# Rotary halves exchanged by transfers, and stacked high and low query parts for the grouped heads, in a two-block transformer kernel

## The chip, the cores and the metric

One core of a Trainium2 chip runs the whole program. The metric is the device time of one execution in microseconds (us). The kernel before takes 2801.74 us, the median of three runs (2801.63 to 2803.39).

## The reference

A sequence of 512 tokens of width 1024 goes through two mixing layers of a first block (`attn0`, `attn1`) and then through six stages of a second block (four gated feed-forward stages, a state-space mixer, a convolution mixer). All is float32. The change touches the attention of the two mixing layers only:

```
proj = rms_norm(x) @ w_in           # split into dq dk dv dgate gq gk gv ggate mq mgate
dq, dk  = rope(dq), rope(dk)        # 6 heads of 2x32, halves of 16 rotated
gq = axial_rope(rms_norm(gq))       # 6 query heads of 64, in groups of 3
gk = axial_rope(rms_norm(gk))       # 2 key heads of 64
def rope(x):  x1, x2 = halves(x); return concat(x1*cos - x2*sin, x2*cos + x1*sin)
oa = softmax(q1 k1') v - lam * softmax(q2 k2') v      # 6 differential heads
ob = softmax(gq gk') v                                # 6 grouped heads
om = softmax(mq mk') mv                               # 4 memory heads, 256 keys
x = x + rms_norm(concat(oa, ob, om) * silu(gates) @ w_out)
```

## The kernel before

**Split products.** Float32 operands of the large products are split into a leading part of reduced precision (type fp32r) and a low part, the difference. A product is the sum of three: high by high, high by low, low by high. `mm3` (lines 418 to 423) issues them for the projections, lines 1949 to 1951 for the scores.

**Projections.** The activations lie with their 1024 features in the partitions (`XH`, `XL`). `w_in` comes in 12 blocks of 256 columns, loaded to two alternating buffers `raw` by SyncE's queue (`load_block`, line 410: the load waits until VectorE has used the buffer). ScalarE writes the leading part `WH` (line 383), VectorE the low part `WL` (line 388), TensorE does 48 products of 512 columns into two banks, and VectorE evicts each bank with the norm factor to a tile of `PR` (lines 2257 and 2259). Blocks are counted two higher in the weight order from the fifth on, since two blocks of `w_mem_kv` come between; so `low_w(12)`, `low_w(13)` and `low_w(14)` on VectorE are the low parts of block 10, block 11 and the first block of `w_out`. Block 11 (the memory queries) is multiplied inside the unit loop, by `queries` in the first five units.

**Rotation.** Ten tiles turn: six of the differential heads (`ROPED[0]` to `[5]`) and, after their norm (`head_norm`, line 2292), the three tiles of grouped queries and one of grouped keys (`ROPED[6]` to `[9]`). TensorE's `swap(n)` (line 1878) multiplies a tile by a permutation that exchanges rows 16 apart and leaves it in bank 6 or 7. VectorE's `turn(n)` multiplies the tile by the cosine (line 2301), the exchanged tile by the signed sine (line 2302), and adds (line 2304). The turns stand between the evictions and the low parts of the weights in VectorE's written order: turns 0 and 1 after `low_w(8)`, 2 and 3 after `low_w(9)`, 4 and 5 after `low_w(10)`, 6 and 7 after `low_w(11)` and the four head norms, 8 and 9 after `low_w(12)`.

**Grouped keys.** Heads whose rows don't match their key head's rows read a copy `gk2` of the keys with the halves changed (lines 2333 and 2334), announced by `ready`. ScalarE's `lead_qk` (line 2112) writes the leading parts of all queries and keys, GpSimd's `low_qk` (line 1820) the low parts.

**Unit loop.** A unit is one head and one tile of 128 queries: 24 differential units (two score sets each), 24 grouped, 16 memory. For each, TensorE makes scores (lines 1949 to 1951), VectorE their maxima (line 2346), ScalarE the exponentials (line 2180), VectorE reciprocals (line 2361), GpSimd scales (lines 1828 and 1830, or 1837), TensorE transposes (line 1978) three units later, ScalarE or VectorE copies to `PT` (lines 2190, 2355), and TensorE multiplies by the values every second unit (line 1992). Every engine runs its part in the written order of units; semaphores tie them. Three norm products stand at unit 42 (line 1959).

Of the kernel before, what the change touches and what calls it, by code (L numbers as in the profile page):

```python
# [96 lines left out]
def program(nc, io, stages=FULL):  # L97
    ctx = ExitStack()
    with ctx:
# [185 lines left out]
        y_scr = nc.dram_tensor("y_scr", [KD, P, CL, NC], F32).ap()  # L285
        tab_scr = nc.dram_tensor("tab_scr", [P, TAB], F32).ap()
        mm_scr = nc.dram_tensor("mm_scr", [12, P, 72, 32], F32).ap()
        z_scr = nc.dram_tensor("z_scr", [3, 4, P // 4, 4, P], F32).ap()
        k_scr = nc.dram_tensor("k_scr", [2, LAGS, P], F32).ap()
        cs_scr = nc.dram_tensor("cs_scr", [KD, P, 2, GS, NC + 1], F32).ap()  # L290
# [45 lines left out]
        def col(name, k, n=0):  # L336
# [8 lines left out]
                        rstd_ok=1, ysq_dve=1, ystat_ok=2, yrms_ok=2, ycol_ok=2, ybc_ok=2, xn=2 * KD),  # L345
            "ffn": dict(silu=KF, hid=KF, hh=KF, hl=KF, ysq_in=9, ysq_use=7, ysq_dve=1),
            "attn": dict(mem_in=32, rope_in=16, mem_n=2, ml=KD, mem_t=KD, mh=KD, mrms=1, msq=2, vm_t=1, vmh=1, vml=1,
                         v_t=4, vh=4, vl=4, gsq=4, gms=4, gln=4, grms=4, gn=4, swapped=10, roped=10, ready=1, gate=8,
                         s=91, e=91, nb=64, p=24, pn=40, rsum=64, scaled=24, qh=14, ql=14, pt=64, pt_a=52, pt_d=12, pv=32, o=16, osq=3, orms=3, og=3,
                         mixh=KD, mixl=KD, ysq_in=8, ysq_use=7, wpart=2),  # L350
            "s5": dict(z=KD, wt=KD, h2=KD, l2=KD, ysq_in=8, ysq_use=7, wpart=2),
            "conv": dict(ysq_in=8, ysq_use=7, wpart=2),
# [1241 lines left out]
        def head(h):  # L1594

            if h < 6:
                parts = [(DQ + h // 2, DK + h // 2, 0, (h % 2) * 64 + 32 * i, 32) for i in range(2)]
                c = (h // 2) * P
                return parts, (lambda s: Vd[:, s, c:c + P]), 4, DG + h // 2
            if h < 12:  # L1600
                g = h - 6
                kv, row = g // 3, (g % 2) * 64
                return ([(GQ + g // 2, GK if kv * 64 == row else "gk2", 0, row, 64)],
                        (lambda s: Vg[:, s, kv, :]), 4, GG + g // 2)
            g = h - 12
            c = (g // 2) * P
            return ([(MQ + g // 2, "MK", (g // 2) * NMEM, (g % 2) * 64, 64)],
                    (lambda s: Vm[:, s, c:c + P]), 2, MG + g // 2)
# [52 lines left out]

        def ms_buf(n):
            return PR[:, (22, 23, 18, 19)[n], :]

        def norm_buf(n):
            return sq[:, n, :] if n < 2 else ssq[:, :]
# [120 lines left out]
        def attn_sp(sp, s):  # L1787
            b0, l = first_block[s], int(s[4])
            wm = io["w_mem_kv"][l].rearrange("(k p) n -> p k n", p=P)
            wi = io["w_in"][l].rearrange("(k p) n -> p k n", p=P)  # L1790

            def in_block(n):
                a = BLOCKS[n][0] * P
                load_block(sp, b0 + n + (2 if n >= 4 else 0), n % 2, raw3(n % 2, KD), wi[:, :, a:a + 2 * P])

            for n in range(4):
                in_block(n)
            if s == stages[0]:
                par_sp(sp, s)
            for q in range(2):  # L1800
                load_block(sp, b0 + 4 + q, q, raw3(q, KD), wm[:, :, q * 256:(q + 1) * 256])
            for n in range(4, 12):
                in_block(n)
            out_sp(sp, b0 + 14, io["w_out"][l])

        def attn_pool(pool, s):
            l = int(s[4])
            if before(s) is None:
                x_all(pool, s)
            pool.dma_start(MEMN[:, :, :], io["mem"][0].rearrange("(t p) d -> p t d", p=P)).then_inc(ss(s, "mem_in"), 16)  # L1810
            pool.dma_start(perm[:, :, :], io["perm_c"]).then_inc(ss(s, "mem_in"), 16)
            squares_pool(pool, s)
            pool.wait_ge(mm_done, first_step[s] + 12)
            pool.dma_start(rope[:, :, :], io["rope_c"]).then_inc(ss(s, "rope_in"), 16)

            def low_qk(n):

                x, high, low, _, _ = SPLIT[n]
                pool.wait_ge(ss(s, "qh"), at(s, "qh", n + 1))
                pool.tensor_tensor(low, x, high.bitcast(F32), ALU.subtract).then_inc(ss(s, "ql"), 1)  # L1820

            for n in range(12):
                low_qk(n)
            for u in range(DIFF_UNITS):
                m = SCORE0[u]
                pool.wait_ge(ss(s, "scaled"), at(s, "scaled", u + 1))
                e1, e2 = E[:, slot(m), :], E[:, slot(m + 1), :]
                pool.tensor_tensor(e2, e2, stats[:, 3, (m + 1) % 8:(m + 1) % 8 + 1].to_broadcast([P, T]), ALU.mult)
                pool.drain()  # L1829
                pool.tensor_tensor(e1, e1, e2, ALU.add).then_inc(ss(s, "p"), 1)  # L1830
                if u in QUERY_ACT:
                    low_qk(12 + QUERY_ACT[u])
            for u in range(DIFF_UNITS, len(UNITS)):
                m, nk = SCORE0[u], HEADS[UNITS[u][0]][2]
                pool.wait_ge(ss(s, "rsum"), at(s, "rsum", u + 1))
                e = E[:, slot(m), 0:nk * P]
                pool.tensor_tensor(e, e, stats[:, 3, m % 8:m % 8 + 1].to_broadcast([P, nk * P]), ALU.mult)\
                    .then_inc(ss(s, "pn"), 1)
            out_pool(pool, s)

        def attn_pe(pe, s):
# [26 lines left out]
                    mm = pe.transpose(bank[4][:, t * P:(t + 1) * P], PR[:, VALUES[n], t * P:(t + 1) * P], ident[:, :])  # L1868
                mm.then_inc(ss(s, "v_t"), 1)

            def swap(n):

                j = ROPED[n][0]
                if j >= GQ:
                    pe.wait_ge(ss(s, "gn"), at(s, "gn", j - GQ + 1))
                if n >= 2:
                    pe.wait_ge(ss(s, "roped"), at(s, "roped", n - 1))
                pe.matmul(bank[6 + n % 2][:, :], perm[:, 0, :], PR[:, j, :], start=True, stop=True)\
                  .then_inc(ss(s, "swapped"), 1)

            in_pair(pe, s, b0, j0)

            def mem_turns(n0, n1):
# [16 lines left out]
                                      ident[:, :])  # L1900
            mm.then_inc(ss(s, "vm_t"), 1)
            pe.wait_ge(ss(s, "mem_in"), at(s, "mem_in", 32))
            swap(0)
            swap(1)
            block(5)
            swap(2)
            swap(3)
            pe.wait_ge(ss(s, "vmh"), at(s, "vmh", 1))
            value_turn(0)
            head_squares(0)  # L1910
            block(6, lambda: head_squares(1))
            swap(4)
            swap(5)
            value_turn(1)
            head_squares(2)
            block(7, lambda: head_squares(3))
            value_turn(2)
            block(8, lambda: (swap(6), swap(7)))
            value_turn(3)
            block(9, lambda: (swap(8), swap(9)))  # L1920
            block(10)
            pe.wait_ge(l_done, b0 + 11 + 2 + 1)
            pe.wait_ge(ss(s, "roped"), at(s, "roped", len(ROPED)))
# [9 lines left out]
            def scores(u):  # L1933
                h, t = UNITS[u]
                if t == 0:
                    pe.wait_ge(ss(s, "ql"), at(s, "ql", 6 if h < 6 else 11 if h < 12 else 14))
                for i, (q, k, k0, row, n) in enumerate(HEADS[h][0]):
                    m = score(u, i)
                    keys = HEADS[h][2] * P
                    (qh, ql), (kh, kl) = [[x[row:row + n, c:c + w] for x in QK[name]]  # L1940
                                          for name, c, w in ((q, t * P, P), (k, k0, keys))]
                    acc = score_bank(u, i)[:, 0:keys]
                    if u >= MEM_U:
                        pe.wait_ge(ss(s, "e"), at(s, "e", m - 2))
                    elif m >= 4:
                        pe.wait_ge(ss(s, "e"), at(s, "e", m - 3))
                    else:
                        pe.wait_ge(acc_read, j0 + min(25 + m, 26))
                    pe.matmul(acc, qh, kh, start=True, stop=False)
                    pe.matmul(acc, qh, kl, start=False, stop=False)  # L1950
                    pe.matmul(acc, ql, kh, start=False, stop=True).then_inc(ss(s, "s"), 1)  # L1951
# [91 lines left out]
        def attn_act(act, s):  # L2043
# [59 lines left out]
            def lead_qk(n):  # L2103
# [5 lines left out]
                    act.wait_ge(ss(s, "ready"), at(s, "ready", 1))  # L2109
                if n >= 12:  # L2110
                    act.wait_ge(acc_read, j0 + 26 + n - 12 + 1)
                act.activation(high, x, ACT.Copy).then_inc(ss(s, "qh"), 1)

            def silu(n):
# [121 lines left out]
        def attn_dve(dve, s):  # L2236
# [25 lines left out]
            def low_w(n):  # L2262
                split_l(dve, b0 + n, n % 2, 16)
# [31 lines left out]
            def turn(n):  # L2295

                j, tab = ROPED[n]
                if n == 0:
                    dve.wait_ge(ss(s, "rope_in"), at(s, "rope_in", 16))
                dve.wait_ge(ss(s, "swapped"), at(s, "swapped", n + 1))  # L2300
                dve.tensor_tensor(PR[:, j, :], PR[:, j, :], rope[:, tab, :], ALU.mult)
                dve.tensor_tensor(work1[:, n % 2, :], bank[6 + n % 2][:, :], rope[:, tab + 1, :], ALU.mult)
                dve.drain()
                dve.tensor_tensor(PR[:, j, :], PR[:, j, :], work1[:, n % 2, :], ALU.add).then_inc(ss(s, "roped"), 1)

            if s == stages[0]:
                par_angle_dve(dve, s)
# [22 lines left out]
            evict(9)  # L2330
            low_w(13)
            dve.drain()
            dve.tensor_copy(gk2[64:128, :], PR[0:64, GK, :])
            dve.tensor_copy(gk2[0:64, :], PR[64:128, GK, :])
            dve.drain()
            dve.nop().then_inc(ss(s, "ready"), 1)
            evict(10)
            low_w(14)

            def maxima(u):  # L2340
# [704 lines left out]
```

## Time and profile before

| what | value |
| --- | --- |
| median of three runs | 2801.74 us |
| the profiled execution's own time | 2802.95 us |
| its span on the core | 2801.1 us |
| TensorE busy (matmul) | 2699.8 us, 96% |
| VectorE busy | 1442.6 us, 51% |
| ScalarE busy | 1099.5 us, 39% |
| GpSimd busy | 697.3 us, 25% |

Times in the views count from the span's start. The layer `attn0` has its projections up to about 193 us and its unit loop to about 360 us; `attn1` projects from about 400 to 566 us and its unit loop begins at 567 us. A busy TensorE in the page is not the same as TensorE at its peak, since matmuls overlap; the distance from start to start tells what one costs. "Chain" below is the view that follows the work which ended last back to what released it.

### The profile page before, as it was taken

How to read it: one execution, taken by the hardware profiler on the slowest of the kernel's cores; microseconds unless marked ns; L12 is line 12 of the kernel's file. 1: busy time of each engine (PE TensorE's matmuls, PEld its weight loads, DVE VectorE, ACT ScalarE, POOL GpSimd, SP SyncE). 2: the span in 40 equal slices, each digit the busy share in tenths (PEclk: the TensorE clock that was granted, in tenths of full speed). 3: DMA queues.
4: the chain of work that ended last, by engine and by line, in shares of the span. 5: the costliest groups of instructions: out<-in, count | busy, mean ns of one | idle time of the engine just before them, and what ended most of it. 6: DMA issues, size and time to landing. Idle time of an engine off the chain costs nothing.

```text
span 2801.1 us, 35940 instructions
## 1 busy us (share of the span) xinstructions
PE 2699.8 (96%) x13734; PEld 2219.0 (79%) x13734; DVE 1442.6 (51%) x1988; ACT 1099.5 (39%) x1787; POOL 697.3 (25%) x601
## 2 busy tenths in 40 slices
PE   6998999999999999999999999999999998999998
PEld 6875688766788888888798888887888886988887
DVE  5566655664475442587364442465432774644423
ACT  3357643376443422423352222342222475422222
POOL 1037430165368700245020000156000200200000
PEclk9999999999999999999999999999999999999999
DMA  3320023200144423444222323345223443232232
GB/s 128 120 76 1 16 69 117 73 31 1 46 92 134 145 77 97 134 136 143 96 76 91 103 76 93 102 165 217 90 83 99 157 149 99 76 101 93 76 94 71
DMA packets 307740, 269.26 MB, mean 96 GB/s; under 512 B 44595, under 2 KB 297948, under 8 KB 304028
## 3 DMA queue, kind: packets, MB, share of 16 engines
q1 hardware_dynamic: 300780, 241.71, 27.9%
q0 software_dynamic: 2800, 20.25, 1.8%
q10 hardware_dynamic: 4032, 5.57, 0.7%
q8 instruction: 82, 1.34, 0.2%
q14 instruction: 46, 0.38, 0.0%
HBM read 239.74 MB, written 27.77 MB: 95 GB/s over the span
## 4 chain that ended last, share of the span: by engine, by line
PE 75%; DVE 7%; POOL 5%; issue 3%; ACT 3%; POOLq 2%; DVEq 2%; SPq 1%; DMA 1%; ACTq 0%
PE bank L421 22%; PE bank L422 22%; PE bank L423 22%; POOL E L1830 2%; POOLq L1829 2%; PE bank L1992 2%; PE bank L1318 2%; DVE XL L481 1%; ACT WH L383 1%; POOL MBB L796 1%; POOL MBA L796 1%; DVE X L585 1%; DVE work L581 1%; DVE WL L388 1%; PE bank L1978 1%
## 5 line engine op out<-in xcount | busy, mean ns | idle before, releaser
L421 PE MATMUL bank<-XH,WH 128*128 128x512 f32 (+1 forms) x2400 | 901.5, 376 | 36.2 <-DVE WL L388 13.6
L422 PE MATMUL bank<-XL,WH 128*128 128x512 f32 (+1 forms) x2400 | 890.9, 371 | 0.0
L423 PE MATMUL bank<-XH,WL 128*128 128x512 f32 (+1 forms) x2400 | 889.3, 371 | 0.0
L388 DVE TENSOR_TENSOR WL<-raw,WH 128x2048 fp32r<-128x2048 f32 (+1 forms) x208 | 443.6, 2133 | 537.2 <-ACT WH L383 536.9
L421 PEld LDWEIGHTS bank<-XH,WH 128*128 128x128 f32 x2400 | 456.1, 190 | 133.5 <-DVE WL L388 18.9
L383 ACT ACTIVATE WH<-raw 128x2048 fp32r<-128x2048 f32 (+1 forms) x208 | 362.5, 1743 | 460.2 <-PE bank L423 459.7
L422 PEld LDWEIGHTS bank<-XL,WH 128*128 128x128 f32 x2400 | 456.8, 190 | 84.6 <-issue 3.3
L423 PEld LDWEIGHTS bank<-XH,WL 128*128 128x128 f32 x2400 | 456.2, 190 | 81.8
L1115 POOL TENSOR_TENSOR ssq<-ssq,sq 128x512 f32<-128x512 f32 x24 | 30.9, 1289 | 1075.3 <-ACT sq L1024 1075.3
L422 PE MATMUL bank<-HL,WH 128*128 128x512 f32 (+1 forms) x792 | 293.9, 371 | 0.0
L423 PE MATMUL bank<-HH,WL 128*128 128x512 f32 (+1 forms) x792 | 293.4, 370 | 0.0
L421 PE MATMUL bank<-HH,WH 128*128 128x512 f32 (+1 forms) x792 | 292.6, 369 | 0.0
L974 ACT ACTIVATE HH<-work 128x512 f32 (+1 forms) x88 | 55.7, 632 | 352.0 <-DVE work L1067 351.6
L422 PEld LDWEIGHTS bank<-HL,WH 128*128 128x128 f32 x792 | 149.0, 188 | 28.6
L421 PEld LDWEIGHTS bank<-HH,WH 128*128 128x128 f32 x792 | 148.7, 188 | 28.9
L423 PEld LDWEIGHTS bank<-HH,WL 128*128 128x128 f32 x792 | 148.8, 188 | 27.1
L2346 DVE TENSOR_REDUCE stats<-bank 128x1 f32<-128x512 f32 (+1 forms) x176 | 108.0, 637 | 113.5 <-PE bank L1951 112.2
L970 ACT ACTIVATE work<-work 128x512 f32<-128x512 f32 x88 | 55.2, 632 | 266.5 <-DVE work L1060 253.6
L1065 DVE TENSOR_TENSOR work<-bank,rstd 128x512 f32<-128x512 f32 x88 | 60.7, 690 | 163.5 <-PE bank L423 161.7
L2180 ACT ACTIVATE E<-bank,stats 128x512 f32<-128x512 f32 (+1 forms) x176 | 113.3, 648 | 78.9 <-DVE stats L2346 78.1
L1060 DVE TENSOR_TENSOR work<-bank,rstd 128x512 f32<-128x512 f32 x88 | 60.1, 686 | 144.8 <-PE bank L423 144.8
L492 POOL TENSOR_TENSOR ssq<-ssq,sq 128x256 f32<-128x256 f32 x112 | 97.4, 870 | 92.5 <-ACT sq L472 87.6
(410 smaller groups left out, 3643.3 us busy)
## 6 DMA issues: line engine op xcount, KB each, us to landing
raw<-in_ffn_w_dram SPq DMA_DIRECT2D x88, 1024.0 KB, 5.3
raw<-in_ffn_w_dram SPq DMA_DIRECT2D x64, 704.0 KB, 4.6
raw<-in_w_in_dram SPq DMA_DIRECT2D x24, 1024.0 KB, 5.2
MM<-mm_scr SPq DMA_DIRECT2D x12, 1152.0 KB, 7.4
raw<-in_w_out_dram SPq DMA_DIRECT2D x8, 1024.0 KB, 5.1
raw<-in_cv_w_in_dram SPq DMA_DIRECT2D x8, 1024.0 KB, 5.5
mm_scr<-MBA POOLq DMA_DIRECT2D x6, 1152.0 KB, 4.7
mm_scr<-MBB POOLq DMA_DIRECT2D x6, 1152.0 KB, 4.5
```

The source lines that it names most:

```text
L383: act.activation(WH[:, slot, 0:n * P], raw[:, slot, 0:n * P], ACT.Copy).then_inc(h_done, 1)
L388: dve.tensor_tensor(WL[:, slot, 0:n * P], raw[:, slot, 0:n * P], WH[:, slot, 0:n * P].bitcast(F32), ALU.subtract).then_inc(l_done, 1)
L421: pe.matmul(out, WH[:, slot, c:c + P], h, start=start, stop=False)
L422: pe.matmul(out, WH[:, slot, c:c + P], l, start=False, stop=False)
L423: return pe.matmul(out, WL[:, slot, c:c + P], h, start=False, stop=stop)
L492: ins = pool.tensor_tensor(ssq[:, HALF[h]], ssq[:, HALF[h]], sq[:, k % 2, HALF[h]], ALU.add)
L796: pool.tensor_tensor(MB[m % SLOTS_M][:, c:c + NQ // 2, :], w[:, c:c + NQ // 2].unsqueeze(2).to_broadcast(shape), EYE[:, :].unsqueeze(1).to ...
L1060: dve.tensor_tensor(work1[:, o, :], bank[o][:, :], rstd[:, :], ALU.mult).then_inc(acc_read, 1)
L1065: dve.tensor_tensor(work1[:, o, :], bank[2 + o][:, :], rstd[:, :], ALU.mult).then_inc(acc_read, 1)
L1318: mm = pe.matmul(bank[4 + k % 3][:, g * NS:(g + 1) * NS], MM[:, m % SLOTS_M, c:c + PH, :].rearrange("p q c -> p (q c)"), PZ[:, n, g, j:j + ...
L2180: act.activation(E[:, slot(m), 0:nk * P], score_bank(u, i)[:, 0:nk * P], ACT.Exp, bias=stats[:, 1, m % 8:m % 8 + 1], accum_out=stats[:, 2, ...
L2346: ins = dve.tensor_reduce(stats[:, 1, c:c + 1], score_bank(u, i)[:, 0:nk * P], AX, ALU.max, negate=True)
```

## The change

Three things are done in both mixing layers.

1. The ten `swap` products leave TensorE. SyncE's queue writes each tile twice, one copy behind the other in each block of 32 rows, to scratch memory in HBM, and reads back the rows that lie 16 further, which is the tile with its halves exchanged, to an SBUF buffer `exchanged(n)`. Tiles 0 to 5 are written after the load of block 4 and read after that of block 5; tiles 6 to 9 are written after the load of block 10 and read, and only then block 11 is loaded. A turn waits until all reads of its set have landed.
2. For the grouped heads, the two 64-row halves of a 128-row tile hold the high part and the low part of one head's queries. One product of 128 rows against keys that are the same in both halves gives high by high plus low by high; one product of 64 rows gives high by low. The keys of both heads are laid out in both halves.
3. The parts for this are made differently: ScalarE copies two half tiles for each grouped query tile, VectorE makes six half-tile differences after the eviction of block 10, GpSimd's three differences go, and VectorE has three key copies for two.

```diff
+        swap_scr = nc.dram_tensor("swap_scr", [10, P // 32, 4, 16, T], F32).ap()
...
+        def exchanged(n):
+            j = (0, 1, 16, 17, 20, 21, 20, 21, 0, 1)[n]
+            return work1[:, j, :] if j < 2 else PR[:, j, :]
...
-            for n in range(4, 12):
+            def swap_out(n):
+                j = ROPED[n][0]
+                if j >= GQ:
+                    sp.wait_ge(ss(s, "gn"), at(s, "gn", j - GQ + 1))
+                else:
+                    sp.wait_ge(acc_read, tiles_before[s] + acc_of(j) + 1)
+                for i in range(2):
+                    sp.dma_start(swap_scr[n, :, 2 * i:2 * i + 2].rearrange("g o c t -> g (o c) t"), PR[:, j, :])\
+                      .then_inc(ss(s, "swap_out"), 16)
+            def swap_in(n):
+                sp.wait_ge(ss(s, "swap_out"), at(s, "swap_out", 32 * (6 if n < 6 else 10)))
+                if n >= 6:
+                    sp.wait_ge(ss(s, "roped"), at(s, "roped", 6))
+                sp.dma_start(exchanged(n), swap_scr[n, :, 1:3].rearrange("g o c t -> g (o c) t"))\
+                  .then_inc(ss(s, "swapped"), 16)
+            in_block(4)
+            for n in range(6):
+                swap_out(n)
+            in_block(5)
+            for n in range(6):
+                swap_in(n)
+            for n in range(6, 11):
                 in_block(n)
+            for n in range(6, 10):
+                swap_out(n)
+            for n in range(6, 10):
+                swap_in(n)
+            in_block(11)
...
-            for n in range(12):
+            for n in (0, 1, 2, 3, 4, 5, 9, 10, 11):
                 low_qk(n)
...
-            swap(0)
-            swap(1)
             block(5)
-            swap(2)
-            swap(3)
...
-            swap(4)
-            swap(5)
...
-            block(8, lambda: (swap(6), swap(7)))
+            block(8)
             value_turn(3)
-            block(9, lambda: (swap(8), swap(9)))
+            block(9)
...
+                    if 6 <= h < 12:
+                        stacked = QK[q][row // 64][:, t * P:(t + 1) * P]
+                        kh, kl = QK[k]
+                        acc = score_bank(u, i)
+                        pe.wait_ge(ss(s, "e"), at(s, "e", m - 3))
+                        pe.matmul(acc[:, :], stacked, kh, start=True, stop=False)
+                        pe.matmul(acc[:, :], stacked[row:row + 64, :], kl[row:row + 64, :], start=False, stop=True)\
+                          .then_inc(ss(s, "s"), 1)
+                        continue
...
+                if 6 <= n < 9:
+                    act.activation(high[0:64, :], x[0:64, :], ACT.Copy)
+                    act.activation(rest(GQ + n - 6)[64:128, :], exchanged(n)[64:128, :], ACT.Copy)\
+                       .then_inc(ss(s, "qh"), 1)
+                    return
...
-                dve.wait_ge(ss(s, "swapped"), at(s, "swapped", n + 1))
+                dve.wait_ge(ss(s, "swapped"), at(s, "swapped", 16 * (6 if n < 6 else 10)))
                 dve.tensor_tensor(PR[:, j, :], PR[:, j, :], rope[:, tab, :], ALU.mult)
-                dve.tensor_tensor(work1[:, n % 2, :], bank[6 + n % 2][:, :], rope[:, tab + 1, :], ALU.mult)
+                dve.tensor_tensor(exchanged(n), exchanged(n), rope[:, tab + 1, :], ALU.mult)
                 dve.drain()
-                dve.tensor_tensor(PR[:, j, :], PR[:, j, :], work1[:, n % 2, :], ALU.add).then_inc(ss(s, "roped"), 1)
+                if 6 <= n < 9:
+                    top, low = slice(0, 64), slice(64, 128)
+                    dve.tensor_tensor(PR[top, j, :], PR[top, j, :], exchanged(n)[top, :], ALU.add)
+                    dve.tensor_tensor(exchanged(n)[low, :], exchanged(n)[low, :], PR[low, j, :], ALU.add)\
+                       .then_inc(ss(s, "roped"), 1)
+                else:
+                    dve.tensor_tensor(PR[:, j, :], PR[:, j, :], exchanged(n), ALU.add).then_inc(ss(s, "roped"), 1)
...
-            dve.tensor_copy(gk2[64:128, :], PR[0:64, GK, :])
+            dve.tensor_copy(gk2[64:128, :], PR[64:128, GK, :])
             dve.tensor_copy(gk2[0:64, :], PR[64:128, GK, :])
+            dve.drain()
+            dve.tensor_copy(PR[64:128, GK, :], PR[0:64, GK, :])
             dve.drain()
             dve.nop().then_inc(ss(s, "ready"), 1)
             evict(10)
+            for n in range(6, 9):
+                x, high, low, _, _ = SPLIT[n]
+                dve.wait_ge(ss(s, "qh"), at(s, "qh", n + 1))
+                dve.tensor_tensor(high[64:128, :], x[0:64, :], high[0:64, :].bitcast(F32), ALU.subtract)
+                dve.drain()
+                dve.tensor_tensor(low[0:64, :], exchanged(n)[64:128, :], low[64:128, :].bitcast(F32), ALU.subtract)\
+                   .then_inc(ss(s, "ready"), 1)
             low_w(14)
```

## Rows read from the trace of the kernel before

**Rows 1.** The page: share of each engine, and TensorE's granted clock in 40 slices.

```profile
PE 2699.8 (96%) x13734; PEld 2219.0 (79%) x13734; DVE 1442.6 (51%) x1988; ACT 1099.5 (39%) x1787; POOL 697.3 (25%) x601
PEclk9999999999999999999999999999999999999999
```

**Rows 2.** The chain in `attn0`: start us, duration us, what (engine, tile, line).

```profile
110.79 1.72 PE bank L1878 x4
...
277.19 0.42 PE bank L1949
...
308.81 0.42 PE bank L1949
```

**Rows 3.** The chain in `attn1`, grouped heads: its first and last score product.

```profile
649.56 0.57 PE bank L1949
...
696.44 0.43 PE bank L1949
```

**Rows 4.** Timeline, grouped unit in `attn0`: start, duration, engine, line, operation, tiles.

```profile
294.90 0.39 PE L1950 MATMUL bank<-PRr,roper 64*128 64x512 f32 x1
295.13 0.39 PE L1951 MATMUL bank<-roper,PRr 64*128 64x512 f32 x1
```

**Rows 5.** Timeline of VectorE in `attn1`, in brackets its idle time before.

```profile
531.56 5.79 DVE L2292 SCALAR_TENSOR_TENSOR PR<-PR,headg 128x512 f32<-128x512 f32 x4
537.27 0.68 DVE L2301 TENSOR_TENSOR PR<-PR,rope 128x512 f32<-128x512 f32 x1
...
541.21 1.31 DVE L2259 TENSOR_TENSOR PR<-bank,rstd 128x512 f32<-128x512 f32 x2
543.84 2.29 DVE L388 TENSOR_TENSOR WL<-raw,WH 128x2048 fp32r<-128x2048 f32 x1 [1.32 <-ACT WH L383]
548.72 0.69 DVE L2301 TENSOR_TENSOR PR<-PR,rope 128x512 f32<-128x512 f32 x1 [2.59 <-PE bank L1878]
...
557.19 2.29 DVE L388 TENSOR_TENSOR WL<-raw,WH 128x2048 fp32r<-128x2048 f32 x1 [1.31 <-ACT WH L383]
559.57 1.34 DVE L2333 COPY gk<-PR 64x512 f32<-64x512 f32 x1
...
566.38 0.69 DVE L2259 TENSOR_TENSOR PR<-bank,rstd 128x512 f32<-128x512 f32 x1 [3.23 <-PE bank L423]
569.42 2.29 DVE L388 TENSOR_TENSOR WL<-raw,WH 128x2048 fp32r<-128x2048 f32 x1 [2.35 <-ACT WH L383]
571.63 2.48 DVE L2346 TENSOR_REDUCE stats<-bank 128x1 f32<-128x512 f32 x4
```

**Rows 6.** Timeline of ScalarE in `attn1`, same columns.

```profile
562.40 0.63 ACT L2112 ACTIVATE roper<-PR 128x512 fp32r<-128x512 f32 x1 [3.69 <-DVEq L2335]
...
567.49 1.90 ACT L383 ACTIVATE WH<-raw 128x2048 fp32r<-128x2048 f32 x1
...
577.79 0.69 ACT L2180 ACTIVATE E<-bank,stats 128x512 f32<-128x512 f32 x1 [1.45 <-DVE stats L2346]
```

**Rows 7.** Timeline of SyncE's queue in `attn1`: issue of the loads of blocks 4 and 11.

```profile
453.31 0.37 SPq L413 DMA_DIRECT2D raw<-in_w_in_dram  x1
...
531.67 0.37 SPq L413 DMA_DIRECT2D raw<-in_w_in_dram  x1
```

**Rows 8.** DMA issues: tile, queue, count, KB each, median us from issue to landing.

```profile
raw<-in_w_in_dram SPq DMA_DIRECT2D x24, 1024.0 KB, 5.2
...
cs_scr<-CSA ACTq DMA_DIRECT2D x8, 520.0 KB, 3.2
...
U<-u_scr SPq DMA_DIRECT2D x8, 256.0 KB, 4.0
YR<-y_scr SPq DMA_DIRECT2D x8, 256.0 KB, 5.6
```

**Rows 9.** VectorE copy SBUF to SBUF elsewhere; GpSimd's differences beside the key copies.

```profile
L1516 DVE COPY ssq<-CV x1: 419/419/419, 2310.6 to 2310.6; 128x512 f32<-128x512 f32 x1
...
557.75 7.01 POOL L1820 TENSOR_TENSOR PRr<-PR,roper 128x512 fp32r<-128x512 f32 x4 [10.47 <-ACT roper L2112]
```

**Rows 10.** Timeline of TensorE in `attn1`: one transpose group of four.

```profile
589.22 1.12 PE L1978 MATMUL bank<-ident,E 128*128 128x128 f32 x4 [1.32 <-POOL E L1830]
...
595.26 0.60 PE L1978 MATMUL bank<-ident,E 128*128 128x128 f32 x4
```

More of the change, by code:

```diff
@@ L347, in program @@
             "attn": dict(mem_in=32, rope_in=16, mem_n=2, ml=KD, mem_t=KD, mh=KD, mrms=1, msq=2, vm_t=1, vmh=1, vml=1,
-                         v_t=4, vh=4, vl=4, gsq=4, gms=4, gln=4, grms=4, gn=4, swapped=10, roped=10, ready=1, gate=8,
-                         s=91, e=91, nb=64, p=24, pn=40, rsum=64, scaled=24, qh=14, ql=14, pt=64, pt_a=52, pt_d=12, pv=32, o=16, osq=3, orms=3, og=3,
+                         v_t=4, vh=4, vl=4, gsq=4, gms=4, gln=4, grms=4, gn=4, swap_out=16 * 20, swapped=16 * 10, roped=10, ready=4, gate=8,
+                         s=91, e=91, nb=64, p=24, pn=40, rsum=64, scaled=24, qh=14, ql=11, pt=64, pt_a=52, pt_d=12, pv=32, o=16, osq=3, orms=3, og=3,
                          mixh=KD, mixl=KD, ysq_in=8, ysq_use=7, wpart=2),
@@ L1602, in head @@
                 kv, row = g // 3, (g % 2) * 64
-                return ([(GQ + g // 2, GK if kv * 64 == row else "gk2", 0, row, 64)],
+                return ([(GQ + g // 2, ("gk2" if kv else GK), 0, row, 64)],
                         (lambda s: Vg[:, s, kv, :]), 4, GG + g // 2)
@@ L1869, in value_turn @@
                 mm.then_inc(ss(s, "v_t"), 1)
[L1871 to L1879, printed above, removed]
             in_pair(pe, s, b0, j0)
@@ L1935, in scores @@
                 if t == 0:
-                    pe.wait_ge(ss(s, "ql"), at(s, "ql", 6 if h < 6 else 11 if h < 12 else 14))
+                    pe.wait_ge(ss(s, "ql"), at(s, "ql", 6 if h < 6 else 8 if h < 12 else 11))
+                    if 6 <= h < 12:
+                        pe.wait_ge(ss(s, "ready"), at(s, "ready", 4))
                 for i, (q, k, k0, row, n) in enumerate(HEADS[h][0]):
@@ L1939, in scores @@
                     keys = HEADS[h][2] * P
+                    if 6 <= h < 12:
+                        stacked = QK[q][row // 64][:, t * P:(t + 1) * P]
[6 more added lines that the diff above has]
+                        continue
                     (qh, ql), (kh, kl) = [[x[row:row + n, c:c + w] for x in QK[name]]
```

## Prediction

> **What bounds the kernel now.** I read the page first: TensorE is busy 96% of the span and the granted clock is 9 tenths or more in every slice [rows 1]. An instruction taken from TensorE is therefore worth its time unless something else ends last where it stood, so each edit needs its own stage. The change lies in the two mixing layers, and I followed the chain there, then each engine's own timeline. The reader sees three regimes. In the projections the chain runs on TensorE; the swaps stand on it, two of them in 1.72 us [rows 2]. From the last projection blocks to the first exponential TensorE isn't the end: the key copies announce `ready`, ScalarE's next leading part starts at once at 562.40 [rows 6], and behind it come the gates, the leading part of the first `w_out` block, VectorE's low part at 569.42 and the first maxima at 571.63 [rows 5, 6]. In the unit loop the differential units go round through all engines (maxima, exponentials, GpSimd, transposes), and the grouped units lie on TensorE's own order: the chain passes 14 grouped score groups in `attn0` [rows 2] and 18 in `attn1` [rows 3] with no other engine between them.
>
> **Part 1, the swap products.** Two swaps cost 1.72 us, so one is 0.86, six are 5.2 and ten are 8.6 us in each layer [rows 2]. The first six go without a price: their tiles are evicted before the load of block 4 is issued at 453.31 [rows 7], the writes are 3 MB and the reads 1.5 MB, and by the rate between transfers of 520 KB in 3.2 us and 1024 KB in 5.2 us (0.25 MB each us; the read and write rows are mixed, so this is cautious) they need 12 and 6 us [rows 8]; turn 0 comes some 35 us after that issue, at 488. The loads of blocks 5 and 6 queue behind them for a few us, and each buffer is refilled well before its turn. If this cover were gone, each us of late data would be a us of TensorE. So TensorE finishes block 7, and everything hung on it, 5.2 us earlier.
>
> **The second exchange.** This is where the cost is. The head norms end where turn 6 now starts, at 537.27 [rows 5]; with the 5.2 us gained, at 532.1. Only then can the last tile be written. Its two issues take 0.37 us each [rows 7]; the write lands after about 2.8 us (520 KB take 3.2 [rows 8]); the four reads are issued over 1.5 us and the last lands 4.0 us later, as reads of 256 KB from scratch do elsewhere [rows 8]. Sum 0.7 + 2.8 + 1.5 + 4.0 = 9.0, less some 0.7 since the last issue overlaps: 8.3 us. Bounds: 6 us if all land as fast as the nearest slopes allow, 12 with the 5.6 us of a contended read [rows 8]. Taken: 8.3. In this time VectorE stands before turn 6, and behind that wait are queued the eviction of block 8, `low_w(12)`, turns 8 and 9, the eviction of block 9, `low_w(13)` and the key copies; block 10 on TensorE waits for two of them. SyncE holds the load of block 11 too, but from 531.67 - 5.2 [rows 7] it moves to about 537 and has until VectorE's `low_w(13)`, some 18 us later.
>
> Step by step, in the time of `attn1`: turn 6 starts at 540.4. A turn is 2.0 us now (turns 6 and 7 with the first eviction start fill 537.27 to 541.21 [rows 5]); turns 6, 7 and 8 get a fourth operation of 0.6, as the last addition is halved by rows and not shortened: 2.6. So 545.6 after turns 6 and 7, 546.9 after the eviction (1.31), 549.1 after `low_w(12)` (2.2). TensorE was done with block 9 at about 545.5 (no swaps in blocks 8 and 9), so it idles 3.6 us: of the 8.6 us, 5 are left, and block 10 ends at 560.3, where it now ends at about 566.4 [rows 5]. VectorE goes on: turns 8 and 9, 553.7; eviction, 555; `low_w(13)`, 557.2, against 559.4 now. 2.2 us of gain.
>
> **Key copies.** They take 1.34 and 1.42 us now, while GpSimd computes its four differences for 7.01 us from 557.75 [rows 5, 9]. A copy of twice the partitions and the same 512 columns takes 0.42 us where GpSimd is idle [rows 9]. Three of the four differences beside them go to VectorE, so GpSimd stands still here: three copies at 0.45 with two drains, 1.7 us, against 3.0 now. Bounds 1.5 and 4.5 us (the old price three times). `ready` comes at 558.9, 3.5 us before 562.40.
>
> The Trainium skill ("GPSIMD Engine Reference", Specifications) says that GpSimd shares its SBUF interfaces with VectorE and that instructions in a two-port mode or with two SBUF inputs contend. By that rule the copies are fast as I take them and the six new differences, which have two SBUF inputs, are slow beside GpSimd; the row of 1.34 us against 0.42 agrees for the copies, and no row shows a half-tile difference.
>
> **Half-tile differences.** Six new VectorE operations follow the eviction of block 10. Their leading parts are ready long before. The price of one is between 0.7 (a whole tile's operation [rows 5]) and 1.4 (a half-tile copy under contention [rows 5]); with GpSimd's three remaining differences overlapping about half, 5.5 us for six with drains; ends 4.3 and 8.4. They start after the second eviction at 561.0, or near 563 if the idle time before block 10 halves TensorE's clock for a while (that this happens after short waits is seen where four transposes take 1.12 us in place of 0.60, right behind a wait of 1.32 [rows 10]). So 566.5 to 568.5, then `low_w(14)` (its ScalarE part starts 5.1 us after `ready` [rows 6], at 564.0, and is in time), and the first maxima at 568.7 to 570.7 in place of 571.63 [rows 5]. Taken: 2 us earlier. ScalarE's three extra half copies (0.5 us each) fall in its idle stretch before `ready`.
>
> **The first units.** `queries` puts 48 products (11.2 us) between the first five units' scores. ScalarE waits 1.45 us for unit 2's maxima at 577.79 [rows 6], because TensorE started the queries only at 566.4. It will start them 3 to 6 us earlier against loop start gained 2, so some of these waits go: 1 us a layer (0 to 2.5).
>
> **Part 2, the score products.** In a grouped unit two following products start 0.23 us apart [rows 4]; one of three goes, and the first, with 128 rows for 64, streams the same 512 columns. TensorE-bound units: 14 + 18 = 32 [rows 2, 3]; 32 x 0.235 = 7.5 us. The other 16 grouped units lie where POOL or, from unit 42 in `attn0`, ScalarE and VectorE end last; nothing there. A pair of units falls from 4.7 to 4.3 us, and ScalarE needs about 3.4 and GpSimd 2.1 of it, so the rest of the ring is still shorter. Bounds 4 and 9.
>
> **Sum.** Two layers x (2 + 1) + 7.5 = 13.5 us. From the profiled execution's 2802.95 us: 2789.5; that execution is 1.2 above the median of the runs, so against the median 2788.2. The exchange is the least certain term and its errors lean to the slow side, so I put it at 2789.
>
> **The DMA page's price.** The Trainium skill ("DMA: Bandwidth & Descriptors", Anatomy of one DMA) gives 2.0 us plus bytes at 436 GB/s for one transfer, most of it the receipt from memory. An estimate from it for the last write and the four reads is 2.6 + 4.4 us, and with the issues 8 us; the sum would stay. It speaks against the change in that no smaller tile makes this shorter.
>
> **Rivals.** (a) *The exchange takes the place of the swaps and more*: with a round trip of 12 us, the upper bound, everything in the start moves 3.7 us later, VectorE's gain of 2 is a loss of 1.7 in each layer, and 7.5 - 3.4 + 2 leaves about 6: 2796. For it: three dependent steps through HBM; against it: the queue is nearly empty then. (b) *Slower*: the same mechanism, with VectorE as its place, decides from a round trip of about 15 us, or from 12 us with the six differences at their upper price (2.9 us more a layer). At a round trip of 16 and that price each layer loses 7.7 + 2.9 - 3 = 7.6 us, against 7.5 for the scores: 2801.7 + 15.2 - 7.5 = 2809. (c) *The score product is hidden*: in the grouped units the ring through VectorE (which has s5's parameters to compute in `attn0`) or ScalarE ends as late as TensorE; the start's 6 us and 2 of the 7.5 are left: 2794. (d) *The exchange is cheap*, under 5 us, and VectorE's chain gives 5 us a layer: 2783, with fewer throttled stretches 2779. (e) *The change doesn't do what it says*: the product of 128 rows costs two of 64; then (c) without the 2, 2796.
>
> **How the numbers follow.** Forecast 0.50 (its own range 2784 to 2795), (a) 0.14, (b) 0.08, (c) 0.14, (d) 0.10, (e) 0.04. The range leaves out (b) and the far end of (d), and adds 3 us for where the halved clock falls: 2780 to 2801. A difference of 0.2%, 5.6 us, is about what a measurement of this kernel can tell from none; faster means under 2796.1. Faster: the forecast nearly whole, (c), (d), a half of (a) and of (e): 0.77. Same: the rest of (a) and (e) and some of the forecast: 0.14. Slower: 0.09.
>
> **What would show it.** In the profile after: no wait of TensorE in blocks 5 to 7; VectorE idle for 8 us before turn 6 with a DMA as releaser; TensorE idle 3 to 4 us before block 10; key copies of 0.4 us; half-tile differences of 0.7 to 1.4; first maxima 2 us earlier; grouped units 0.47 us a pair shorter on the chain. The prediction is wrong if TensorE waits in blocks 5 to 9 for a weight load (SyncE stuck behind an exchange), if the round trip is over 12 us, or if the chain in the grouped units leaves TensorE.

## The result, and the profile after

The changed kernel takes 2895.97 us, the median of four runs, against 2801.68 us of the kernel before beside it: a ratio of 1.0338, 95% interval 1.0325 to 1.035. Forecast were 2789 us, with a range of 2780 to 2801. The change makes the kernel 94 us slower.

The page after: the span, the shares of the engines, TensorE's busy tenths and its granted clock in 40 slices of 72 us.

```profile
span 2893.1 us, 35852 instructions
...
PE 2688.9 (93%) x13646; PEld 2216.7 (77%) x13646; DVE 1453.8 (50%) x2008; ACT 1103.2 (38%) x1793; POOL 681.7 (24%) x595
...
PE   6777999759999999999999999999999998999998
...
PEclk9888999889999999999999999999999999999999
```

The row of busy tenths before:

```profile
PE   6998999999999999999999999999999998999998
```

TensorE has 10.9 us less work than in [rows 1] and the span is 92 us longer. The new low digits are slices 2 to 4 and slices 8 and 9: one stretch in each of the two mixing layers. There the granted clock falls to 8 tenths too.

Who waits for whom, between 60 and 260 us (engine, tile and line that waited, what released it: us in total, times, longest):

```profile
ACT WH L384 <- DMA raw<-in_w_in_dram: 73.2, 3, 32.2
...
DVE WL L389 <- ACT WH L384: 46.5, 8, 24.9
DVE PR L2338 <- DMA work<-swap_scr: 34.5, 1, 34.5
PEld bank L422 <- DVE WL L389: 31.7, 2, 30.9
```

VectorE stands 34.5 us before turn 6, which was forecast at 8.3. But ScalarE also waits three times, 73.2 us in all, for plain loads of `w_in`; before, this line waited in these 200 us for TensorE alone. The first two of these waits, for blocks 5 and 6, hold up the projections (the third, 32.2 us for block 11, lies beside VectorE's own wait):

```profile
121.90 1.91 ACT L384 ACTIVATE WH<-raw 128x2048 fp32r<-128x2048 f32 x1 [22.58 <-DMA raw<-in_w_in_dram]
142.23 1.91 ACT L384 ACTIVATE WH<-raw 128x2048 fp32r<-128x2048 f32 x1 [18.42 <-DMA raw<-in_w_in_dram]
...
126.24 0.77 PE L422 MATMUL bank<-XH,WH 128*128 128x512 f32 x1 [15.34 <-issue]
```

The last row is block 5 on TensorE, which had no product for the 15.3 us before it. SyncE's queue shows where the loads stood. The 12 writes of the first exchange are issued from 79.56 to 107.94 us (start, duration, engine, line, operation, tiles, count; the two rows are from two views, and their counts overlap):

```profile
79.56 17.66 SPq L1817 DMA_DIRECT2D swap_scr<-PR  x9
94.78 13.15 SPq L1817 DMA_DIRECT2D swap_scr<-PR  x4
```

The first three writes are issued in 0.5 to 0.9 us each and the next five in 2.3 to 3.0, and not in 0.37 us as the load in [rows 7]. By the view of the line over the whole run (shortest, median and longest issue in ns) the median is 2443 ns:

```profile
L1817 SPq DMA_DIRECT2D swap_scr<-PR x40: 502/2443/5727, 79.6 to 612.8; - x40
```

The load of block 5 stands behind 12 of these. And in a stretch where writes alone move (columns: window, its length, busy time of the five engines, granted clock, DMA share, GB/s):

```profile
84.00:90.00 6.00, 6.00 (x41) 5.41 (x40) 1.25 (x2) 1.92 (x1) 0.00 (x0) 1.00 0.26 102
```

a quarter of the 16 DMA engines' time is used, and 102 GB/s is moved. 256 KB at 102 GB/s are 2.57 us: after the first three, a write is issued about as slowly as the data pass. I read this as a full queue. The share of a quarter gives the suspicion that the experiments on the exchange turn on: the transfer's view has 4 blocks of 32 rows outermost, and 4 engines work.

### The profile page after: what moved, and what is told of

It is laid out like the page before. It is cut to its first block, busy times and chain, and to the rows that moved or that the text cites. A ratio compares the mean times of both kernels' runs of the same rounds, so it can differ in the third digit from the quotient of the medians.

```text
span 2893.1 us, 35852 instructions
## 1 busy us (share of the span) xinstructions
PE 2688.9 (93%) x13646; PEld 2216.7 (77%) x13646; DVE 1453.8 (50%) x2008; ACT 1103.2 (38%) x1793; POOL 681.7 (24%) x595
## 4 chain that ended last, share of the span: by engine, by line
PE 69%; DVE 8%; DMA 5%; POOL 5%; issue 4%; SPq 3%; ACT 3%; DVEq 2%; POOLq 2%; ACTq 0%
PE bank L422 20%; PE bank L424 20%; PE bank L423 20%; POOL E L1867 2%; PE bank L2024 2%; DMA swap_scr<-PR 2%; POOLq L1866 2%; PE bank L1319 2%; SPq L1817 1%; DVE WL L389 1%; ACT WH L384 1%; DMA raw<-in_w_in_dram 1%; POOL MBB L797 1%; DVE XL L482 1%; POOL MBA L797 1%
## 5 line engine op out<-in xcount | busy, mean ns | idle before, releaser
L2217 ACT ACTIVATE E<-bank,stats 128x512 f32<-128x512 f32 (+1 forms) x176 | 113.4, 648 | 73.3 <-DVE stats L2398 72.7
```

The lines of the kernel that those rows point to most:

```text
L2217: act.activation(E[:, slot(m), 0:nk * P], score_bank(u, i)[:, 0:nk * P], ACT.Exp, bias=stats[:, 1, m % 8:m % 8 + 1], accum_out=stats[:, 2, ...
```

## The experiments

**Theory A**: the outermost dimension of a transfer's view sets how many engines carry it. **Theory B**: writing to scratch in HBM and reading back is slow by bytes and receipts. Where a ratio and its interval stand, the time is the median of several executions, against the kernel before beside them; a time marked "one execution" is just that. A layer below is one of the two mixing layers.

### The exchange in a flat layout

```diff
-swap_scr = nc.dram_tensor("swap_scr", [10, P // 32, 4, 16, T], F32).ap()
+swap_scr = nc.dram_tensor("swap_scr", [10, 2, P, T], F32).ap()
-sp.dma_start(swap_scr[n, :, 2 * i:2 * i + 2].rearrange("g o c t -> g (o c) t"), PR[:, j, :])
+sp.dma_start(swap_scr[n, i], PR[:, j, :])
-sp.dma_start(exchanged(n), swap_scr[n, :, 1:3].rearrange("g o c t -> g (o c) t"))
+sp.dma_start(exchanged(n), swap_scr[n, 1])
```

> The changed kernel with the same bytes in the same number of transfers, but a flat scratch layout: each tile is written twice as 128 rows one behind the other and read back as 128 rows, so that no transfer has a view of 4 blocks outermost. The halves are not exchanged (that part of the computation is left out). Theory A: a view whose outermost dimension is 4 is dealt to 4 of the 16 DMA engines; then here the DMA share rises from 0.25 to near 1 while exchanges run, one write of 256 KB takes under 1 us in place of 2.45 us, the two waits of 20 to 35 us for an exchange shrink to 8 us at most, and the time is 2785 to 2800 us, the forecast that was made for the change. Theory B: writing to scratch in HBM and reading it back is slow in itself, by bytes and receipts; then writes stay at 2.45 us each and the time stays within 10 us of 2896.

The loops and semaphores around these lines stay as they are; the kernel leaves out the exchange of the halves. Measured: 2794.86 us, ratio 0.9979 (0.9970 to 0.9989). The line of the writes, and a stretch in which they run:

```profile
L1817 SPq DMA_DIRECT2D swap_scr<-PR x40: 320/462/1517, 79.5 to 528.8; - x40
...
86.00:91.00 5.00, 5.00 (x41) 4.82 (x39) 2.32 (x2) 1.92 (x1) 0.00 (x0) 1.00 1.04 400
```

The same 256 KB are issued in 0.46 us (median) and pass at 400 GB/s, with a DMA share of 1.04. 101 us are gone, with the same bytes, receipts and number of transfers. Theory B falls. The wait before turn 6 is 10.4 us in the first layer and 10.1 in the second, over the 8 expected at most.

### The same addresses, cut by blocks

```diff
+for g in range(4):
+    sp.dma_start(swap_scr[n, g, 2 * i:2 * i + 2].rearrange("o c t -> (o c) t"), PR[32 * g:32 * g + 32, j, :])
```

(and the reads likewise, one for each block of 32 rows).

> The changed kernel with the same addresses and bytes, but each exchange transfer cut in four, one for each block of 32 rows, so that the outermost dimension of each is 32 rows. 80 writes and 40 reads a layer in place of 20 and 10. Theory A (outermost dimension of 4 uses 4 engines): all 16 engines carry each piece; the data of one tile passes in under 1 us, and the limit becomes the issue of 0.37 us for each piece: 18 us for the first writes (30 now), 3 + 2 + 6 + 2 = 13 us for the second exchange (35 to 40 now): 2800 to 2825 us. Theory B (HBM scratch or its addresses are slow): the pieces take together as long as now, and with the receipts of four times as many the time is 2896 us or more.

Measured: 2836.53 us, one execution: 59 us less than with whole tiles at the same addresses, so the addresses in HBM aren't the cause. It is over the expectation of 2800 to 2825, though. The pieces are issued at 0.43 us (median) and not at 0.37; the 48 writes of the first exchange take 25.5 us and not 18. In the second exchange 26 of the 32 writes are still to go 1.3 us before the last norm ends, at 0.52 us each:

```profile
164.94 13.49 SPq L1818 DMA_DIRECT2D swap_scr<-PR  x26
```

VectorE waits 22.2 us before turn 6 in the first layer, against 13 expected. The number of transfers is a price of its own. This run also tells issue from data: here the load of block 5 is issued at 105.32 us, 2.7 us earlier than in the changed kernel, and ScalarE has its block at 111.22, 5.9 us later; in the changed kernel that takes from 107.98 to 121.90, 13.9 us. So a load behind the writes waits for its issue and then, it seems, for data of the writes before it.

### One write in place of two

```diff
-for i in range(2):
-    sp.dma_start(swap_scr[n, :, 2 * i:2 * i + 2]..., PR[:, j, :])
+sp.dma_start(swap_scr[n, :, 0:2]..., PR[:, j, :])
```

> The changed kernel with one write for each tile in place of two, in the same pattern of 4 blocks outermost; the read takes the same rows back, so the halves are not exchanged (left out). Both theories have the write time fall with the bytes; it tells how the loss hangs on the length of the exchange. 10 writes of 2.45 us fewer in each layer: the first writes end about 15 us earlier, the second exchange 5 to 10 us earlier. If the loss is the time that the queue and VectorE stand behind the exchanges, each layer wins 20 to 25 us: 2846 to 2856 us. If only one of the two exchanges mattered, half of that: about 2870.

(The read takes the same rows back, so the exchange is left out.)

Measured: 2841.41 us, one execution: 54.6 us less, 27 in each layer. This is 4.6 us beyond the expected range, on the side of a loss that follows the length of both exchanges. In the first layer the head norms come 15.7 us earlier (161.88 us) and the wait before turn 6 is 9.8 us shorter (24.7 us).

### 8 and 2 blocks outermost

```diff
+swap_scr = nc.dram_tensor("swap_scr", [10, K, 3 * 128 // K, T], F32).ap()      # K = 8, K = 2
+sp.dma_start(swap_scr[n, :, R * i:R * i + R], PR[:, j, :])                      # R = 128 // K
```

> The changed kernel with a scratch layout whose view has 8 blocks of 16 rows outermost in place of 4 of 32 (same bytes, same number of transfers; the halves aren't exchanged, left out). Theory A, one engine for each outermost index: 8 engines work, a write of 256 KB takes 1.2 us in place of 2.45 and the DMA share is 0.5 while exchanges run; the loss, about 100 us at 4 engines and none at 16, falls to a third or less: 2800 to 2835 us. If what mattered is only whether the view is flat, it stays near 2896.

> The same with 2 blocks of 64 rows outermost (halves not exchanged, left out). Theory A: 2 engines, 4.9 us for a write of 256 KB, DMA share 0.125 while exchanges run. 20 writes and 10 reads a layer take 147 us in place of 74, so up to 73 us more in each layer: 3020 to 3045 us. If the share and the time stay as with 4 blocks, theory A is wrong.

Both leave the exchange out; the reads take the first `R` rows of each block. Measured: 2814.50 us with 8 and 3042.80 us with 2, one execution each. The stretch from 86 to 91 us, where all kernels write, with 8 blocks and then with 2:

```profile
86.00:91.00 5.00, 5.00 (x41) 4.82 (x40) 2.37 (x2) 1.92 (x1) 0.00 (x0) 1.00 0.53 204
```

```profile
86.00:91.00 5.00, 5.00 (x36) 4.63 (x36) 1.48 (x2) 1.92 (x1) 0.00 (x0) 1.00 0.13 51
```

Rates of 51, 102, 204 and 400 GB/s for 2, 4, 8 and 128 rows or blocks outermost, at shares of 0.13, 0.26, 0.53 and 1.04. Sixteen times the share is 2.1, 4.2, 8.5 and 16.6: for 2, 4 and 8, one engine for each outermost index, at 25.5 GB/s each. Theory A holds for these sizes; others under 16 were not run, and the count of engines is read from the share, since the views don't tell which engines worked. The Trainium skill ("DMA: Bandwidth & Descriptors", Rules for kernel authors, "Use all 16 engines") says that the slowest dimension of the views sets the number of engines and that a size under 16 confines the whole transfer to at most so many. All four rows agree with it. The prediction drew on this page for the fixed cost of a transfer alone, and that figure stands there for transfers that GpSimd issues, where these are SyncE's.

### The scores alone, and their product priced

The ten swaps are TensorE's again, no transfer is made, the stacked queries and all that belongs to them stay:

```diff
-dve.tensor_tensor(exchanged(n), exchanged(n), rope[:, tab + 1, :], ALU.mult)
+dve.tensor_tensor(exchanged(n), bank[6 + n % 2][:, :], rope[:, tab + 1, :], ALU.mult)
```

> Part 2 alone: the ten permutation products are back on TensorE and no transfer is made; the stacked queries, the two score products, the half-tile differences and the key copies are as in the changed kernel. Forecast's terms: the 32 grouped units on TensorE's order win 0.235 us each, 7.5 us; the start of the unit loop wins 1 to 3 us by faster key copies and loses up to 4 us by six differences in each layer. Theory 1 (the score term was right): 2790 to 2797 us. Theory 2 (the rest of the ring ends as late, the product was hidden): 2798 to 2806.

Measured: 2794.26 us, ratio 0.9975 (0.9965 to 0.9984). Then the second product was issued once more in that kernel:

```diff
+pe.matmul(acc[:, :], stacked[row:row + 64, :], kl[row:row + 64, :], start=False, stop=False)
 pe.matmul(acc[:, :], stacked[row:row + 64, :], kl[row:row + 64, :], start=False, stop=True)
```

> The kernel with part 2 alone, with its second score product of 64 rows issued twice in each grouped unit, so three products again (the scores are then wrong: the high by low term counts twice; nothing is left out). It prices the product by itself. Forecast's term: 32 units on TensorE's order, 0.235 us each, 7.5 us: 2794.3 + 7.5 = 2801.8, between 2798 and 2804. If the product was hidden, within 2 us of 2794.3.

Measured: 2800.35 us, ratio 0.9996 (0.9986 to 1.0006). Against the kernel before beside each, the first is 7.1 us faster and the second 1.2: one product of three in the grouped units is worth about 5.9 us, where 7.5 were forecast. The two intervals only just don't overlap, but the traces say the same: it wasn't hidden. In the first layer the first maxima come at the same time in both (199.63 and 199.61 us), and the norm products of unit 42 at 309.33 and 312.69:

```profile
309.33 1.88 PE L1976 MATMUL bank<-sq,perm 128*128 128x512 f32 x4
```

```profile
312.69 1.88 PE L1977 MATMUL bank<-sq,perm 128*128 128x512 f32 x4
```

3.4 us, and 14 products at 0.235 are 3.3. In the second layer the same stretch, from the first maxima to unit 42, is 108.7 against 112.1 us: 3.5 us, where 18 products (4.2 us) were forecast.

### Which exchange costs what

The first exchange as in the changed kernel, the second by TensorE:

```diff
-for n in range(6, 10): swap_out(n)
-for n in range(6, 10): swap_in(n)
+pe.matmul(bank[6 + n % 2][:, :], perm[:, 0, :], PR[:, j, :], start=True, stop=True)    # n = 6 to 9
```

> The first exchange as in the changed kernel (through scratch, 4 blocks outermost), the second by TensorE. It splits the loss. By the place of the head norms in the first layer (177.6 us in the changed kernel, 153.0 in the flat one) the first exchange costs 24.6 us a layer, and by the stretch from the norms to the first maxima (70.1 against 46.1) the second 24. So this kernel should lie about 20 us a layer above the one with the scores alone: 2830 to 2838 us, with the head norms at 177 to 178 us. The prediction had put this exchange at no price: then 2784 to 2795.

Measured: 2837.24 us, one execution, with the head norms at 177.96 us. It lies 43 us above the scores alone, about as expected, and 53 us above the version below in which the same six tiles are exchanged by direct transfers. So the exchange that the prediction put at no price costs as much as the one it feared.

### Direct transfers

Pairs of tiles move from SBUF to SBUF, 16 rows at a time, with no scratch. First all ten tiles go this way, then six of them with the other four on TensorE. Both do the whole exchange.

```diff
+for k in range(8):
+    a, b = 16 * k, 16 * (k ^ 1)
+    sp.dma_start(to[a:a + 16], PR[b:b + 16, first:first + 2, :])
```

> All ten tiles by direct transfers from SBUF to SBUF, 40 of 64 KB a layer, with no scratch. The second exchange has one receipt in place of two. In the flat version the wait before turn 6 is 10.1 us; here pair 6 and 7 can start after two norms, and the last 8 transfers are issued in 3 to 4 us and land 2 us later: the wait before turn 6 falls to 3 to 6 us, and the key copies come 4 to 7 us earlier than in the flat version. Forecast 2784 to 2791 us. If the wait stays near 10 us, the round trip was not what cost it, and the time is 2795.

Measured: 2787.67 us, ratio 0.9950 (0.9934 to 0.9967). The wait before turn 6 (in brackets, last row) is 4.9 us:

```profile
152.37 5.85 DVE L2317 SCALAR_TENSOR_TENSOR PR<-PR,headg 128x512 f32<-128x512 f32 x4
163.15 0.69 DVE L2329 TENSOR_TENSOR PR<-PR,rope 128x512 f32<-128x512 f32 x1 [4.93 <-DMA PR<-PR]
```

> The six tiles of the differential heads are exchanged by direct transfers from SBUF to SBUF, 16 rows of two tiles each (24 transfers of 64 KB a layer, none with a view of 4 outermost), the four of the grouped heads by TensorE as before the change; stacked scores as in the changed kernel. Theory A says that the first exchange is hidden when it isn't bound to 4 engines: TensorE reaches the head norms 5.2 us earlier in each layer than in the kernel with the scores alone (157.44 us in the first layer there, so 152.3 here), and no VectorE wait stands before turn 6: 2794.3 - 10.3 = 2784 us, 2780 to 2788. If instead the many small transfers stand in the loads' way, the head norms come no earlier and it is 2794 or more.

Measured: 2784.34 us, ratio 0.9940 (0.9924 to 0.9957), the fastest of all and faster than both kernels. Against the scores alone, the norms start 5.4 us earlier in the first layer, and the first maxima too (199.63 there):

```profile
152.04 5.78 DVE L2323 SCALAR_TENSOR_TENSOR PR<-PR,headg 128x512 f32<-128x512 f32 x4
...
194.24 2.48 DVE L2395 TENSOR_REDUCE stats<-bank 128x1 f32<-128x512 f32 x4
```

Against the version with all ten direct it is 3.3 us faster, but the intervals of the two ratios overlap, so their order is likely and not shown.

## Why the prediction was wrong

**The step that failed** is the first term of the exchange, "the first six go without a price". It took a rate of 0.25 MB each us from transfers whose views have 128 rows outermost, and an issue of 0.37 us from a load into an empty queue. The changed kernel moves 0.10 MB each us, and after the first three SyncE stands about 2.4 us at each write. The 12 writes take 28.4 us, and the load of block 5, behind them, is issued 16 us late (107.98 in place of 91.7 us in the flat version). ScalarE's part of that block's weights starts at 121.9 (99.15 in the flat version), VectorE's ends at 126.1, and only then does TensorE go on. The load of block 6 stands behind the six reads as well, which go out when all writes have landed (119.10 us): its part on ScalarE starts at 142.2 in place of 110.5. Two of the prediction's own signs of being wrong came with it, TensorE waiting in blocks 5 to 9 for a weight load and a round trip over 12 us. Compared with the flat version by VectorE's first head norm in the first layer, here the changed kernel and then the flat version:

```profile
177.62 5.85 DVE L2329 SCALAR_TENSOR_TENSOR PR<-PR,headg 128x512 f32<-128x512 f32 x4
...
218.00 0.69 DVE L2338 TENSOR_TENSOR PR<-PR,rope 128x512 f32<-128x512 f32 x1 [34.52 <-DMA work<-swap_scr]
...
247.73 2.48 DVE L2398 TENSOR_REDUCE stats<-bank 128x1 f32<-128x512 f32 x4
```

```profile
153.00 5.85 DVE L2327 SCALAR_TENSOR_TENSOR PR<-PR,headg 128x512 f32<-128x512 f32 x4
...
199.09 2.48 DVE L2396 TENSOR_REDUCE stats<-bank 128x1 f32<-128x512 f32 x4
```

the first exchange costs 24.6 us (177.62 against 153.00), and from there to the first maxima the second costs 24.0 (70.1 against 46.1). In the second layer the same two are 26.2 and 24.7. Together they are 99.5 us, of 102.7 between the spans of the two traces and 101 between the medians. The rest, 3.2 us, lies in the first layer's stretch from the first maxima to the norms of unit 42 (112.1 against 108.9 us), where the mean granted clock is 0.92 against 0.94. In the second layer, after as long a wait before turn 6 (34.7 us), both have 0.94 and the stretch is 108.9 against 108.8. So this rest goes with the clock; why the clock was lower in the first layer alone stays open.

**The second exchange**: the place, the mechanism and what waits behind it were as written, the size was not. Forecast was a round trip of 8.3 us with an upper bound of 12; it is 34.5. The eight writes are issued from 179.43 us, and the first read, which waits until all have landed, at 203.50, 24.1 us later (8.6 in the flat version; eight writes at 2.57 us are 20.6). Turn 6 starts 14.5 us after that read's issue (5.8 in the flat version; four reads at that rate would be 10.3). Rival (b), slower by this very mechanism from 15 us on, is what came, at a chance of 0.08 and a price of 2809 us. Its price fell short because it, too, kept the rate and left the first exchange out.

**All other steps can be read in the flat version**, in which the transfers pass at 400 GB/s, faster than was assumed. It came to 2794.9 where 2789 was forecast: 6.5 us faster than the kernel before, of 12.7 forecast. The scores alone bring 7.1, so the exchange was worth about nothing even at this rate. Its trace lies 2.7 us below its median and that of the kernel before 1.2 above its own, so up to 4 us of a difference between the two traces belong to the executions.

- TensorE's six swaps: head norms 5.13 us earlier (153.00 against 158.13), forecast 5.2. Right.
- Round trip: 10.4 and 10.1 us, forecast 8.3, bounds 6 to 12. Within the bounds, a size off by about 2 us a layer.
- Key copies: 0.42 us each for 1.34 and 1.42 [rows 5], with GpSimd idle beside them, forecast 0.45. Right.
- Half-tile differences: 0.69 us each, the lower bound, in place of 0.92 taken. In the second layer GpSimd's three differences had all but ended when they began (561.37 against 561.23 us), so their price beside GpSimd stays open (one in the changed kernel that began 0.4 us before GpSimd ended took 0.90). But they start at 561.2 in a run in which the projections of `attn1` begin 4.2 us earlier than before (the load of block 4 is issued at 449.12 in place of 453.31), which answers to 565.4; forecast was 561 to 563. TensorE's block 10 is the cause. Its first products:

```profile
547.26 0.79 PE L422 MATMUL bank<-XH,WH 128*128 128x512 f32 x1 [6.02 <-DVE WL L389]
547.85 0.63 PE L423 MATMUL bank<-XL,WH 128*128 128x512 f32 x1
```

It waits 6.0 us and not 3.6, and then starts products 0.43 us apart, at a granted clock of 0.50 from 547 to 550 us (0.23 at the higher level [rows 4]), so that the block ends at 560.5, after 13.2 us in place of 11.2. The prediction named this clock and took a value between the two ends.
- First maxima: 0.8 us earlier in the first layer (199.09 against 199.93). In the second, for which the forecast was worked out, they come at 567.88; with the 4.2 us this answers to 572.1, 0.4 us later than before (571.63 [rows 5]). Forecast was 2 us earlier in each. So the start of the unit loop gave 0.4 us over both layers in place of 4. In the second layer the longer round trip (1.8 us) and the slower block 10 (2.0 us), less 1 us for the cheaper differences, roughly make the loss.
- Grouped units: the products' distance is as forecast. A pair of units goes from 4.7 to 4.3 us in the chain of the flat version:

```profile
278.93 0.59 PE bank L2008 x4
279.52 0.23 PE bank L1966
279.75 0.43 PE bank L1967
280.18 1.92 PE bank L2022 x8
...
283.20 0.59 PE bank L2008 x4
```

The 128-row product (L1966) now stands right behind the transposes at 0.23 us and the step to 64 rows (L1967) takes 0.43, where the first 64-row product took that before. The whole stretch from the first maxima to unit 42 is 108.9 us in place of 113.4 in the first layer (4.5; forecast 3.3 and 1). In the second it is 108.8 in place of 117.3 (8.6; forecast 4.2 and 1). There the version with three products has 112.1, so 3.5 us are the product, and what the other 5 are stays open.

So one number, the rate, made the change a loss, and it stood under two terms. It wasn't the only one that was off: with the rate right, half of the forecast gain came. In the recorded working one step also doesn't close: of the 8.6 us of swaps 5 are left after the 3.6 of idle time, but the end of block 10 is moved from 566.4 to 560.3, which is 6.1. The bounds of the unknown rate were drawn from rows of other transfers, none of which had so small an outermost dimension, and no sentence asked whether those rows were of the same kind.

## What to carry to other kernels

Before a transfer is priced by other transfers, compare their views: with 2, 4 or 8 indices outermost it had as many engines' worth of rate as indices here, and its price was multiplied. Put rows or partitions outermost, or cut and regroup the transfer so that they are; here, 16-row pieces of two tiles each, from SBUF to SBUF, did the same exchange without scratch. Price a queue by what stands behind each transfer when the queue is full. Move only the work that has cover: the six early tiles gained 5 us a layer, and the four late ones paid with a wait what TensorE had saved.

## What the runs showed of the hardware

- A write of 256 KB from SBUF to HBM on SyncE's queue moved 51, 102, 204 and 400 GB/s with 2, 4, 8 and 128 indices outermost. Its issue took 5.0, 2.44, 0.86 and 0.46 us (medians; the first few of a row are shorter, with 8 blocks 0.6 to 0.7 us and then 1.1 to 1.6).
- With 4 blocks outermost the issue was about as slow as the data from the fourth write on (2.3 to 3.0 us for the next five, against 2.57), and SyncE's next instruction, a plain load, waited too: 2.38 us of issue at 107.98 us, in place of 0.37.
- Pieces of 64 KB cost 0.43 us of issue as a median in place of 0.37 for a 1 MB load, and 0.52 in a row of 26.
- A copy of 64 rows by 512 columns on VectorE took 0.42 us with GpSimd idle and 1.34 and 1.42 beside its differences.
